# x as the stationary operand of the SSD decay-matrix products, two heads side by side in the PE array, and the state term added after its turn

## What is computed

```python
def ssd_scan(x, dt, a, b, c, h0):          # per direction, per chunk of 128 tokens
    cb = jnp.einsum('bclgn,bcsgn->bgcls', cc, bc)
    wmat = cb[:, :, None] * _segsum_exp(a_cum)
    y_diag = jnp.einsum('bghcls,bcsghp->bclghp', wmat, xd)
    ...
    y_off = jnp.einsum('bclgn,cbghpn->bclghp', cc, h_prev) * decay_out[..., None]
    y = (y_diag + y_off).reshape(bsz, L, H, P)
...
def finish(y, xs, z, ref):
    y = y + xs.astype(jnp.float32) * d_skip.astype(jnp.float32)[:, None]
    y = rmsnorm(y * jax.nn.silu(z.astype(jnp.float32)), gnorm_w)
    return (y @ w_out).astype(ref.dtype)
```

## Time and profile before

| | |
|---|---|
| time, median of 3 runs | 1393.86 us (1393.27 to 1397.33) |
| span of the profiled execution, first to last instruction | 1395.9 us |
| PE matmul busy | 1232.0 us, 88% of the span |
| PE weight load busy | 743.7 us, 53% |
| DVE busy | 928.7 us, 67% |
| ACT busy | 581.8 us, 42% |
| POOL busy | 116.5 us, 8% |
| mean granted TensorE clock | 0.942 of full |

### The profile page before, as it was taken

One profiled execution on the slowest core, in us unless ns is written; L12 is line 12 of the kernel. 1 busy time (PEld: TensorE's weight loads), 2 busy tenths in 40 slices (PEclk: granted clock), 3 DMA queues, 4 the chain that ended last, 5 costly groups with the idle time before them and its releaser, 6 DMA issues.

```text
span 1395.9 us, 20639 instructions
## 1 busy us (share of the span) xinstructions
PE 1232.0 (88%) x7274; PEld 743.7 (53%) x7274; DVE 928.7 (67%) x1445; ACT 581.8 (42%) x1005; POOL 116.5 (8%) x127
## 2 busy tenths in 40 slices
PE   7679988988988768969999999997999977799997
PEld 7335554554554543424444444443765535688886
DVE  5984674674665568988788788564527755755654
ACT  2344543553653434323433333222334544456642
POOL 0003024014015110000000000000000000000000
PEclk9989989989989969979999999998999997899998
DMA  9213102202202033634564554522222100355552
GB/s 391 89 56 106 61 16 92 73 15 79 86 31 91 1 121 112 225 145 181 183 238 183 187 227 155 218 85 89 91 91 91 60 30 31 122 212 207 181 196 106
DMA packets 24957, 172.88 MB, mean 124 GB/s; under 512 B 2768, under 2 KB 2768, under 8 KB 6608
## 3 DMA queue, kind: packets, MB, share of 16 engines
q1 hardware_dynamic: 19008, 129.28, 25.4%
q0 software_dynamic: 5184, 37.75, 7.4%
q10 hardware_dynamic: 720, 5.24, 1.0%
HBM read 171.22 MB, written 1.05 MB: 123 GB/s over the span
## 4 chain that ended last, share of the span: by engine, by line
PE 49%; DVE 10%; issue 2%; ACT 2%; DMA 0%; DVEq 0%; ACTq 0%; POOL 0%; SPq 0%
PE bank L1284 14%; PE bank L1285 14%; PE bank L1286 14%; PE bank L1569 1%; DVE arena L756 1%; DVE arena L803 1%; PE bank L1583 1%; DVE arena L798 1%; PE bank L1556 1%; PE bank L1558 1%; PE bank L1557 1%; ACT wh L390 1%; DVE arena L1014 1%; DVE hl L794 1%; PE bank L1576 1%
## 5 line engine op out<-in xcount | busy, mean ns | idle before, releaser
L1284 PE MATMUL bank<-hh,wh 128*128 128x512 f16 (+1 forms) x1152 | 399.8, 347 | 38.4 <-DVE hl L794 19.3
L726 DVE SCALAR_TENSOR_TENSOR wl<-raw,wh 128x1024 f16<-128x1024 f32 (+1 forms) x232 | 269.0, 1177 | 237.5 <-ACT wh L390 235.5
L1285 PE MATMUL bank<-hl,wh 128*128 128x512 f16 (+1 forms) x1152 | 399.2, 347 | 0.0
L1286 PE MATMUL bank<-hh,wl 128*128 128x512 f16 (+1 forms) x1152 | 398.8, 346 | 0.0
L390 ACT ACTIVATE wh<-raw 128x1024 f16<-128x1024 f32 (+1 forms) x232 | 229.9, 1011 | 288.8 <-PE bank L1286 219.1
L1284 PEld LDWEIGHTS bank<-hh,wh 128*128 128x128 f16 x1152 | 114.8, 100 | 147.8 <-issue 62.0
L1284 PE MATMUL bank<-arena,wh 128*128 128x512 f16 (+1 forms) x544 | 182.0, 335 | 10.9 <-DVE wl L726 3.8
L1285 PE MATMUL bank<-arena,wh 128*128 128x512 f16 (+1 forms) x544 | 181.9, 334 | 0.0
L1286 PE MATMUL bank<-arena,wl 128*128 128x512 f16 (+1 forms) x544 | 181.8, 334 | 0.0
L756 DVE SCALAR_TENSOR_TENSOR arena<-arena,araw 128x1024 bf16<-128x1024 f32 x144 | 167.6, 1219 | 0.2
L1286 PEld LDWEIGHTS bank<-hh,wl 128*128 128x128 f16 x1152 | 114.3, 99 | 95.7 <-issue 6.6
(11 more groups left out here) (194 smaller groups left out, 1451.5 us busy)
## 6 DMA issues: line engine op xcount, KB each, us to landing
raw<-wgu SPq DMA_DIRECT2D x44, 1024.0 KB, 4.8
arena<-wadaT POOLq DMA_DIRECT2D x36, 1024.0 KB, 5.1
raw<-wdn SPq DMA_DIRECT2D x16, 896.0 KB, 4.6
raw<-wxg SPq DMA_DIRECT2D x8, 1024.0 KB, 4.8
raw<-wz SPq DMA_DIRECT2D x8, 1024.0 KB, 4.8
raw<-wout SPq DMA_DIRECT2D x8, 1024.0 KB, 4.8
raw<-wdn SPq DMA_DIRECT2D x8, 1024.0 KB, 4.8
raw<-wqk SPq DMA_DIRECT2D x8, 1024.0 KB, 4.8
```

What stands on the lines that cost most here:

```text
L726: ve.scalar_tensor_tensor(wl[:, u.slot, a:b], raw[:, u.slot, a:b], WS, wh[:, u.slot, a:b], ALU.mult, ALU.subtract).then_inc(lo_done, 1)
L1284: pe.matmul(o, wh[:, u.slot, wsl], ahi[:, k, t0:t1], start=st, stop=False)
L1285: pe.matmul(o, wh[:, u.slot, wsl], alo[:, k, t0:t1], start=False, stop=False)
L1286: i = pe.matmul(o, wl[:, u.slot, wsl], ahi[:, k, t0:t1], start=False, stop=en)
```

## The change

- `within` takes x as the stationary operand (64 columns) and lets E move (128 columns). The output has features on partitions: an even head writes partitions 0 to 63 of YB, an odd head partitions 64 to 127, in the same 128 columns, so that two heads lie in different halves of the array's columns.
- YB is then already turned. DVE's new `from_chunk` adds YB and the skip term into `gt`. It stands at the start of the next chunk's `chunk`.
- The state term alone goes through `ys` and the turn. DVE's new `off` makes it, and stands after E(c,0) and the convolution tile beside it, ahead of E(c,1). With one direction (chunks 0 and 1) L926 writes `ys` directly.
- `y_turn(c)` moves from hook 6 of chunk c+1 to hook 6 of chunk c (for c < 3), and y_turn(3) stays behind `within(3, 1)`. It waits for `off(c)` and, for the bank AB, for the new `from_state(c-1)`.
- DVE's new `from_state(c-1)` adds AB to `gt` and releases POOL; it stands right after `off(c)`.

```diff
@@ DVE @@
+            def from_chunk(g, c):
+
+                ve.wait_ge(yd, g * 8 + (2 * c + 4))
+                if c == 0:
+                    ve.wait_ge(xD_ok, g * QT + QT)
+                ve.wait_ge(g_ok, g * NCH + (c + 1))
+                ve.tensor_tensor(gt[:, c % 2, :].rearrange("p (q l) -> p q l", q=QT), YB[:, :].rearrange("p (q l) -> p q l", q=QT),
+                                 xD[:, :, c * P:(c + 1) * P], ALU.add).then_inc(yb_ok, 1)
+
+            def from_state(g, c):
+
+                ve.wait_ge(a_mm, g * A_PER + (A_YT[c] + 3))
+                ve.wait_ge(yb_ok, g * NCH + (c + 2))
+                ve.tensor_tensor(gt[:, c % 2, :], gt[:, c % 2, :], AB[:, :], ALU.add).then_inc(a_free, 1)
+
             def chunk(g, c, between=None):
 
                 if c == 0:
                     ve.wait_ge(o_free[1], g * O_PER + (O_CB[1] + 2))
+                else:
+                    from_chunk(g, c - 1)
                 for q in range(2):
...
                     if between and q in between:
                         between[q]()
-                parts = []
+                    if q == 0:
+                        off(g, c)
+                        if c:
+                            from_state(g, c - 1)
+
+            def off(g, c):
+
+                one = len(YOFF[c]) == 1
                 for d in sorted(YOFF[c]):
                     f = YOFF[c][d][1]
-                    dst = (ya, yb)[d]
+                    dst = ys[:, c % 2, :] if one else (ya, yb)[d]
                     ve.wait_ge(o_mm[d], g * O_PER + (f + 1))
                     ve.tensor_tensor(dst.rearrange("p (h f) -> p h f", h=HG), wide(OB[d]), per_head(DOUT, c, d), ALU.mult).then_inc(o_free[d], 1)
                     ve.wait_ge(o_free[d], g * O_PER + (f + 2))
-                    parts.append(dst)
-                if len(parts) == 2:
-                    ve.tensor_tensor(ya, ya, yb, ALU.add).then_inc(yp, 1)
-                    ve.wait_ge(yp, g * 2 + (c - 1))
-                ve.wait_ge(yd, g * 8 + (2 * c + 4))
-                ve.tensor_tensor(ys[:, c % 2, :], parts[0], YB[:, :], ALU.add).then_inc(y_ok, 1)
-
-            def skip(g, c):
...
+                if not one:
+                    ve.tensor_tensor(ys[:, c % 2, :], ya, yb, ALU.add).then_inc(y_ok, 1)
...
                 chunk(g, 1, {0: lambda: conv_tile(g + 1, 0), 1: lambda: cvt(u.plus(5))} if more else None)
-                skip(g, 0)
                 chunk(g, 2, {0: lambda: conv_tile(g + 1, 1), 1: lambda: cvt(u.plus(6))} if more else None)
-                skip(g, 1)
-                chunk(g, 3, {0: lambda: (conv_tile(g + 1, 2) if more else None, skip(g, 2))})
+                chunk(g, 3, {0: lambda: conv_tile(g + 1, 2)} if more else None)
                 if more:
                     conv_tile(g + 1, 3)
                 ada_out(g + ADA_FIRST, g * A_PER + A_ADA)
-                skip(g, 3)
+                from_chunk(g, 3)
+                from_state(g, 3)
@@ PE @@
                     if hq == 0:
-                        pe.wait_ge(y_ok, g * NCH + (c + 1))
+                        pe.wait_ge(yb_ok, g * NCH + (c + 1))
                     for h in range(4):
                         hs = slice((4 * hq + h) * HP, (4 * hq + h + 1) * HP)
-                        i = pe.matmul(YB[:, hs], E[:, hq, 0, h, :], xt[:, c, hs], start=(hq == 0 and h == 0), stop=True,
-                                      skip_group_check=True)
+                        rows = slice((h % 2) * HP, (h % 2) * HP + HP)
+                        q = 2 * hq + h // 2
+                        i = pe.matmul(YB[rows, q * P:(q + 1) * P], xt[:, c, hs], E[:, hq, 0, h, :], start=True, stop=True)
                     i.then_inc(yd, 1)
...
                 def y_turn(c):
 
-                    pe.wait_ge(y_ok, g * NCH + (c + 2))
+                    if len(YOFF[c]) == 1:
+                        for d in YOFF[c]:
+                            pe.wait_ge(o_free[d], g * O_PER + (YOFF[c][d][1] + 2))
+                    else:
+                        pe.wait_ge(y_ok, g * 2 + (c - 1))
                     pe.wait_ge(a_free, g * A_PER + (A_YT[c] + 1))
...
-                    return {0: first, 1: last_chunk, 2: second, 4: third, 6: lambda: y_turn(c - 1) if c else None}
+                    return {0: first, 1: last_chunk, 2: second, 4: third, 6: lambda: y_turn(c) if c < 3 else None}
```

More of the change, by code:

```diff
@@ L278, in build @@
         d_mm, e_ok, t_ok, yd = sem("d_mm"), sem("e_ok"), sem("t_ok"), sem("yd")
-        yp, y_ok = sem("yp"), sem("y_ok")
+        yb_ok, y_ok = sem("yb_ok"), sem("y_ok")
         a_mm, a_free = sem("a_mm"), sem("a_free")
@@ L818, in residual @@
                     i.then_inc(xup, 1)
-            for s, n in [(lo_done, LO), (conv_ok, 2), (o_free[0], 1), (o_free[1], 1), (y_ok, 1), (a_free, 1), (a32_ok, 2),
+            for s, n in [(lo_done, LO), (conv_ok, 2), (o_free[0], 1), (o_free[1], 1), (yb_ok, 1), (a_free, 1), (a32_ok, 2),
                          (al_ok, 2), (qkr_ok, 1), (w_ok, 2), (xup, 4)]:
@@ L1258, in _ @@
             group(NG - 1, False)
-            po.wait_ge(y_ok, NG * NCH + 1)
+            po.wait_ge(yb_ok, NG * NCH + 1)
             for b in range(2):
```

## The result

The changed kernel took 1380.93 us in the median of 4 runs (1379.01 to 1384.11). The kernel before, on the same chip, took 1395.0 (4 runs, 1393.27 to 1397.33). The forecast was 11.8, and 1382.0. The gain does not sit where the forecast put it, though: in this profile the steady groups gave next to nothing, the last group twice what was expected.

What follows compares the result with a forecast made beforehand. The prediction took DVE's chain over the group boundary, on which PE waits, to bound the kernel. Three steady groups at -2.2 us (-6.5) and the tail (-5.3) gave -11.8 on 1393.86: 1382.0 us, range 1373 to 1390.

Steps and rivals of the forecast that it cites:

- Boundary (a): End of each steady group: with additions moved, DVE's chain from E(3,0) to the x turn gets 4.9 us shorter.
- Chunk 1 (b): Steady groups: chunk 1's turn waits for DVE's additions behind conv 0, costing PE 1.85 us on the path.
- The fall: Chunk 1's new wait: clock at half for 3.4 us, 1.1 a group, 1385.3; one of three smaller-gain ways, together 0.25.
- the sign that the prediction names itself: The forecast's own condition for being wrong: the wait in chunk 1 of a steady group brings a half clock.
- the gain holds, and more of it: Rival: PE isn't stopped in chunks 1 and 2, 7.2 us more gained, 1374.8; chance 0.14.
- Chunk 2 (c): Steady groups: chunk 2's turn also waits for DVE's additions, 0.55 us with the semaphore.
- Chunk 0 (d): Steady groups: chunk 0 gets a turn it had not, some 0.44 us of PE's stream, on the path.
- Few calls lie on the path: Of the 32 `within` calls, only within(0,0) in a steady group and some six in the tail set the time.
- Last group (e): Tail without convolutions: `ada` starts 4.2 us earlier, YB addition leaves the chain, `within` loses some 0.3; together 5.3 us.
- the heads don't overlap: Rival: `within` costs 0.43 us more on some nine path calls, 1385.9; one of three smaller-gain ways, together 0.25.
- Boundary only 2.8: Rival: 2.8 of 4.9 us comes, E(3,1) staying put, 1388.3; one of three smaller-gain ways, together 0.25.
- The long fall of the clock in chunk 1: Slower-or-nothing rival: 10.2 us at half clock behind the wait, 4.5 a group, 1395.5; slower 0.08, no change 0.13.

Runs made afterwards that it cites:

- k1: The changed kernel's new operands, with DVE's steps and the turns in the old order in all four groups: 1387.54 us, 0.9939 of the kernel before.
- k5: The changed kernel with the new order in the last group alone, the old order in the three steady groups: 1380.72 us, 0.9891 of the kernel before.
- k4: The changed kernel with the new order in the three steady groups alone, the old order in the last: 1388.88 us, 0.9946 of the kernel before.
- the second execution: The changed kernel, unaltered, built and profiled once more: 1380.43 us, 0.9883 of the kernel before.
- k2: The changed kernel with `off` and `from_state` ahead of the convolution in chunks 1 and 2: 1370.38 us, 0.9817 of the kernel before.
- k2b: The changed kernel with `off` and `from_state` ahead of the convolution in chunk 1 alone: 1371.92 us, 0.9824 of the kernel before.
- k7: The changed kernel with all four heads written to YB's lower 64 partitions, half the products missing from the output: 1384.45 us, 0.9922 of the kernel before.
- k3: The changed kernel with the four heads of a call in the order 0, 2, 1, 3: 1380.28 us, 0.9892 of the kernel before.

## Why the total was right and its parts were not

The runs split the gain so: 8.5 us from the operands (k1), 6.7 from the new order in the last group (k5 less k1), and nothing, within an uncertainty of some 3 us, from the new order in the steady groups (k4 against k1, and the changed kernel against k5). I had forecast, by the terms of the working, under 1 for the operands, 5.0 and 6.2. The sum held by luck: the new order in the steady groups gave 6 us less than forecast, the operands 8 more and the order in the last group 2 more.

**Boundary (a): right.** 5.0 us were measured (33.77 to 28.80) for 4.9. Conv 3 starts 7.26 us behind within(3,0) instead of 12.31. The wait at the turn is 2.15 us where I had about 1 (1.24 in the second execution), and the one ahead of the x turn 3.37, where I let 4.2 stay.

**Chunk 1 (b): the mechanism right, the size too small.** This is the step that failed in the steady groups. It had 1.85 us for the wait. The wait is 2.32, since the cheaper `within` brings PE there sooner, and the clock falls behind it, for 3.4 or 6.8 us: together 3.8 to 5.0. The fall was among the rivals, at 3.4 us and 1.1 a group, and it came; I had put the forecast on its not coming, and by the sign that the prediction names itself (a half clock behind the wait in chunk 1) it was wrong here. k2 and k2b show the place: without the wait the fall is gone, and the time is 1370.38, below even the rival "the gain holds, and more of it" at 1374.8.

**Chunk 2 (c): hidden.** No wait in the changed kernel, where PE comes 4.2 us late from chunk 1, and 1.8 us in k2b, where it comes in time.

**Chunk 0 (d): smaller.** The first piece is 10.51 with the turn and 10.33 without (k1): 0.18, for 0.44 in the working.

**"Few calls lie on the path": wrong.** This is the step that failed for the operands. I named one chain, DVE's over the boundary, and counted within(0,0) in a steady group. But in chunks 0 to 2 it is PE's stream that sets the pace, and all six calls there shorten it (k1, 0.14 each). For the last group I let the loop run "by the same durations", so a cheaper `within` saved nothing there but 0.3 at its end: the six calls up to within(3,0), with a 3.4 us stretch of half clock that is gone, save 2.4 us together (k1), and `ada` starts 2.7 us sooner.

**Last group (e): the term was half of what it measured.** `ada` in k1, and then in after, with the two rows that follow it:

```profile
478.48 6.96 PE L1333 MATMUL bank<-s,araw 128*128 128x2 f32 x32 [0.87 <-DVE arena L922]
...
480.65 5.32 PE L1322 MATMUL bank<-s,araw 128*128 128x2 f32 x32 [0.93 <-DVE arena L922]
485.90 1.12 PE L1439 MATMUL bank<-arena 128*64 128x128 f32 x8
486.95 1.12 PE L1461 MATMUL bank<-kp,arena 128*128 128x128 f32 x4
```

From within(0,0), `ada` starts at 24.64 us instead of 31.53, 6.9 sooner, for a forecast of 4.2. The loop's last block, within(3,0), comes 27.46 - 22.29 = 5.2 us sooner; k1 has it at 25.06, so 2.4 are the operands, and 2.8 the order, for which the working had 3.0. The other 1.7 lie between it and `ada`, where the working had 1.2. Against k1, whose `ada` starts 28.84 us behind within(0,0), the order alone brings it 4.2 sooner, just what the working had: what it left out are the operands' 2.7. (Its own terms of the last group, 4.2, 0.7 and 0.3, add up to 5.2, not 5.3.) Then `ada` takes 5.32 us instead of the 6.96 of the earlier trace rows, because it begins 1.85 us before the clock falls. In the second execution, where it falls behind `ada`, it took 3.71; with the `within` behind it, which then starts at full clock, that is nearly all of the 2.0 us between the two last groups. within(3,1) takes 1.12 instead of 1.95, 0.8 less for a forecast of 0.3. These two (1.6 and 0.8) and the YB addition (0.7) are 3.1 of the 3.5 us by which the stretch from `ada` to the sum of squares is shorter.

**Rivals.** That the heads don't overlap is excluded by the 0.385 us of a call, and k7 shows what it would look like. "Boundary only 2.8" is excluded by the boundary's 5.0. The long fall of the clock in chunk 1 (10.2 us) didn't come; 6.8 was the longest.

**Open.** Where and for how long the clock falls differs between executions of one program: in chunk 1 of group 1 from 264.0 us for 3.4 or from 258.6 for 6.8, at the x turn behind it from 322.0 for 6.8 or from 320.1 for 3.4. The two profiled spans of the changed kernel differ by 5.1 us (1382.4 and 1377.3). What decides it was not tried. It differs between the groups of one execution too: the second piece of group 0 is 21.04 us in the first and 19.67 in the second. The 2.5 us behind the scan, where PE has the same instructions, is no more than such a difference: in the profiles of k1 to k7, of k2b and of the second build this part takes 887.4 to 891.8 us, and 888.3 and 890.8 are those of after and before. The split above rests on medians for that reason.

## What to carry to other kernels

Price an edit once for each stretch and its own bound: a chain that sets a group's end doesn't make the in-order stream ahead of it free, and a saving of 0.14 us per call counted in every chunk. When an addition that PE waits for is moved, put it ahead of the long work of its engine and not behind it (k2: four lines, 10 us), and count the slower clock behind a new wait beside the wait. A right total says little about its terms; two half-way kernels, each with one part of the change, told more than the sum.

## What the runs showed of the hardware that was not expected

- The waits of 2.3 us at chunk 1's turn were followed by a stretch at half clock in all twelve steady groups of the four profiles that have them (the changed kernel twice, k3, k4): for 3.4 us in five, for 6.8 in seven. In the second execution of the changed kernel the fall of group 1 (258.6) even comes before the 0.84 us of idle time that follow the turn. In k2, where only the 0.84 is left, no fall followed in chunk 1.
- Shorter waits mostly had none behind them: 1.46 us at the same turn in k7 (none in two groups, 3.4 us in the third), 1.75 us at chunk 2's turn in k2b (none in three).
- Two column halves of the array overlap whatever the order of issue: 0.392 us for a call in the order 0, 2, 1, 3 against 0.385 in the order 0, 1, 2, 3, and 0.81 when all heads lie in one half.
- Getting into and out of the split costs 0.25 us of a call of 0.68, of which 0.09 are ahead of its first record; with all heads in one half it is 0.24 of 1.10.
